# One encoder layer on one core: attention with the values as weights, probabilities scaled before they are transposed, and the modulation pieces spread over two tiles

## What is computed

```python
mod = silu(c) @ ada_w + ada_b                    # 6 x 1024: shift, scale, gate, twice
h = modulate(rms_norm(x, norm1_g), sh1, sc1)
proj = h @ w_in
y_rwkv = rwkv7_time_mix(...)                     # 8 heads of 64, a recurrence over the tokens
y_att = swa_sink_attention(q, k, v, ...)         # 8 query heads, 2 key/value heads of 64
x = x + gt1 * (concatenate([y_rwkv, y_att]) @ w_out)
h2 = modulate(rms_norm(x, norm2_g), sh2, sc2)
x = x + gt2 * hier_moe(h2, ...)                  # 32 experts, two for each token
```

```python
logits = q @ k.T * HEAD_DIM ** -0.5 + bias
probs = softmax(concatenate([logits, sink]))[..., :KEY_BAND]
out = probs @ v
```

## Time and profile before

| | us |
|---|---|
| median of 3 runs | 2782.31 (2781.85 to 2783.21) |
| the profiled execution, its own time | 2783.43 |
| its span in the trace | 2781.5 |
| TensorE busy | 2444.3 (88%) |
| VectorE busy | 1126.3 (40%) |
| ScalarE busy | 755.4 (27%) |
| pass 1 ends, pass 2 begins (from the span's start) | 914.5, 922.8 |

### The profile page before, as it was taken

One profiled execution on the slowest core, in us unless ns is written; L12 is line 12 of the kernel. 1 busy time (PEld: TensorE's weight loads), 2 busy tenths in 40 slices (PEclk: granted clock), 3 DMA queues, 4 the chain that ended last, 5 costly groups with the idle time before them and its releaser, 6 DMA issues. The chain is left out here.

```text
span 2781.5 us, 67296 instructions
## 1 busy us (share of the span) xinstructions
PE 2444.3 (88%) x27710; PEld 1536.3 (55%) x27711; DVE 1126.3 (40%) x2596; ACT 755.4 (27%) x1815; POOL 391.6 (14%) x481
## 2 busy tenths in 40 slices
PE   3999999999997789999999997379999999998970
PEld 1878778788785567677777774223332333232220
DVE  0355645645556245555555554411111111111118
ACT  0244344353443113232323231012122212122212
POOL 0111111111111012121212120001010111110100
PEclk8999999999998799999999998589999999999985
DMA  8012111121123722222222221475535386999959
GB/s 324 9 51 87 47 70 68 47 85 53 46 84 124 305 99 86 101 86 101 86 101 86 101 86 39 185 314 226 219 136 224 138 324 239 384 363 412 373 228 362
DMA packets 54675, 451.78 MB, mean 162 GB/s; under 512 B 7932, under 2 KB 8992, under 8 KB 32576
## 3 DMA queue, kind: packets, MB, share of 16 engines
q1 hardware_dynamic: 36504, 390.71, 35.7%
q0 software_dynamic: 10656, 38.80, 3.6%
q10 hardware_dynamic: 7304, 19.19, 1.9%
HBM read 367.41 MB, written 87.56 MB: 164 GB/s over the span
## 5 line engine op out<-in xcount | busy, mean ns | idle before, releaser
L1729 PE MATMUL ps<-arena 128*32 128x512 f32 x4608 | 510.3, 599 | 27.9 <-DMA arena<-wex 27.9
L1729 PEld LDWEIGHTS ps<-arena 128*32 128x32 f32 x4608 | 150.0, 111 | 381.6 <-issue 358.0
L454 PE MATMUL ps<-arena 128*128 128x128 f32 x3072 | 354.2, 276 | 2.2 <-ACT arena L596 2.1
L454 PEld LDWEIGHTS ps<-arena 128*128 128x128 f32 x3072 | 348.7, 192 | 13.3 <-ACT arena L596 13.3
L1090 PE MATMUL ps<-arena 64*64 64x64 f32 x8704 | 295.2, 220 | 28.6 <-ACT arena L1293 9.2
L1090 PEld LDWEIGHTS ps<-arena 64*64 64x64 f32 x8704 | 275.2, 135 | 57.9 <-issue 56.5
L1743 PE MATMUL ps<-arena 128*32 128x512 f32 x2304 | 268.3, 607 | 15.0 <-DMA arena<-wex 14.1
L1235 PE MATMUL ps<-arena 128*128 128x512 f32 x512 | 238.2, 609 | 0.7 <-ACT arena L1312 0.7
L1951 DVE TENSOR_TENSOR arena<-arena,ps 128x256 f32<-128x256 f32 x72 | 30.0, 416 | 462.5 <-ACT arena L1787 462.5
L465 PE MATMUL ps<-arena 128*128 128x512 f32 (+1 forms) x512 | 216.4, 561 | 0.0
L1787 ACT ACT_TABLE_LOAD x36 | 46.2, 1283 | 592.1 <-PE ps L1729 592.1
(11 more groups left out here) (327 smaller groups left out, 3017.2 us busy)
## 6 DMA issues: line engine op xcount, KB each, us to landing
arena<-wex SPq DMA_DIRECT2D x105, 2048.0 KB
mid<-arena SPq DMA_DIRECT2D x16, 2568.0 KB, 8.5
arena<-mid SPq DMA_DIRECT2D x16, 2568.0 KB, 9.7
arena<-ada SPq DMA_DIRECT2D x12, 2048.0 KB, 10.4
arena<-y SPq DMA_DIRECT2D x16, 1024.0 KB, 8.0
arena<-x SPq DMA_DIRECT2D x31, 512.0 KB, 5.3
arena<-w_in SPq DMA_DIRECT2D x8, 1232.0 KB, 24.8
arena<-x ACTq DMA_DIRECT2D x17, 512.0 KB, 10.8
```

Of the source, the lines that this page charges most:

```text
L454: mm = pe.matmul(bank[name][0:m, at:at + P], V["w_in"][:, kk, w0:w0 + m], V["hT"][:, kk, :], start=(kk == 0), stop=(kk == KD - 1))
L1729: mm = pe.matmul(bank[("HA", "HB")[g]][rows[j], :], xT[:, kk, rows[j]], slot[j][:, at:at + 2 * FH], start=(kk == 0), stop=(kk == KD - 1))
```

## The change

It has four parts.

1. **Values as weights.** In `att5_g` the values (128 keys by 64) are the weights, and the transposed probabilities of two heads (256 columns) stream through. Two heads go to partitions 0 to 63 of C2, two to partitions 64 to 127. There are 4 matmuls for each group, and the result already stands transposed. Pass 2 therefore no longer transposes `ya`: ScalarE copies it straight into `W["yT"]`. The rows of w_out are reordered on the host to fit.
2. **Probabilities scaled first.** The new step `pn_g` on VectorE adds, takes reciprocals and scales the 4 x 192 exponentials of a group in place. `att4_g` waits for it instead of for `probs`. `att4_0` now stands right behind the logits of group 1, ahead of `in_q1`.
3. **Modulation in two rounds.** `mod0` and `mod1` stay in round -1; `mod2` to `mod8` stand in round 0, between the inversion steps of tile 1.
4. **The hand-over.** Pass 1 ends without waiting for its last store. The second ada piece's load and VectorE's first write for `mod0` wait for it instead. w_out is loaded behind the second piece.

```diff
-             ("tok1", 0), ("exp_0", 0), ("in_kv2", 1), ("ev_v", 1), ("tok2", 0), ("ev_l", 1), ("att3_1", 0), ("exp_1", 0),
-             ("in_q1", 1), ("turn_l", 1), ("att4_0", 0), ("in_q2", 1), ("att5_0", 0), ("ev_lora", 1), ("norm", 2),
+             ("tok1", 0), ("exp_0", 0), ("in_kv2", 1), ("ev_v", 1), ("tok2", 0), ("pn_0", 0), ("ev_l", 1), ("att3_1", 0), ("att4_0", 0), ("pn_1", 0), ("exp_1", 0),
+             ("in_q1", 1), ("att5_0", 0), ("turn_l", 1), ("in_q2", 1), ("ev_lora", 1), ("norm", 2),
...
-            sp.wait_ge(S["zero_row"], 16)
-            sp.wait_ge(S["stored"], 16 * nt)
...
-                    S.wait(pe, "probs", 2 * t + g + 1)
+                    S.wait(pe, "pn", 2 * t + g + 1)
...
-                    for i in range(4):
-                        h = 4 * g + i
-                        B.wait_read(pe, f"T{i // 2}", f"P{g}", t)
-                        for part in range(2):
-                            v = V["qkv"][b if part else 1 - b][:, 640 + 64 * g:704 + 64 * g]
-                            mm = pe.matmul(bank["C2"][:, 64 * h:64 * h + 64], V["PT"][:, i, P * part:P * part + P], v,
+                    for half in range(2):
+                        B.wait_read(pe, f"T{half}", f"P{g}", t)
+                    for part in range(2):
+                        v = V["qkv"][b if part else 1 - b][:, 640 + 64 * g:704 + 64 * g]
+                        for half in range(2):
+                            mm = pe.matmul(split(bank["C2"][64 * half:64 * half + 64, 256 * g:256 * g + 256], 2), v,
+                                           V["PT"][:, 2 * half:2 * half + 2, P * part:P * part + P],
                                            start=(part == 0), stop=(part == 1))
...
+            def probs(g):
+                def go(t, b):
+                    S.wait(dve, "probs", 2 * t + g + 1)
+                    g4 = slice(4 * g, 4 * g + 4)
+                    dve.tensor_tensor(V["den"][:, g4], V["sm"][:, g4], V["es"][:, g4], ALU.add)
+                    dve.drain()
+                    dve.reciprocal(V["den"][:, g4], V["den"][:, g4])
+                    dve.drain()
+                    keys = V["Pm_v"][:, :, 64:256]
+                    dve.tensor_tensor(keys, keys, per_channel(V["den"][:, g4], KEYS), ALU.mult).then_inc(S["pn"], 1)
+                return go
...
-                dve.tensor_tensor(split(pk["ya"], QH), split(bank["C2"][:, :], QH), per_channel(V["den"], HD), ALU.mult).then_inc(S["ya"], 1)
+                dve.tensor_copy(pk["ya"], bank["C2"][:, :]).then_inc(S["ya"], 1)
...
+    MODS_FIRST = 2
+
+    def once(step, at):
+        return lambda n, b: step() if n == at else None
 
     def mods(step):
-        return {f"mod{i}": once(lambda i=i: step(i)) for i in range(MODS + 1)}
+        return {f"mod{i}": once(lambda i=i: step(i), 0 if i < MODS_FIRST else 1) for i in range(MODS + 1)}
...
-            for n in range(2):
-                load_ada(sp, S, W["ada"], ins, MOD1 + n)
+            load_ada(sp, S, W["ada"], ins, MOD1)
+            sp.wait_ge(S["stored"], 16 * nt)
+            load_ada(sp, S, W["ada"], ins, MOD1 + 1)
+            sp.dma_start(W["w_out"], ins["w_out"].rearrange("(k p) n -> p k n", p=P)).then_inc(S["w_out"], 16)
...
-                for name, src in (("O1", pk["ya"]), ("O0", W["yc"])):
-                    B.wait_free(pe, name, "yT", t)
-                    if name == "O0":
-                        S.wait(pe, "yr", t + 1)
-                    for c in range(CC):
-                        mm = pe.transpose(bank[name][:, P * c:P * c + P], src[:, P * c:P * c + P], ident)
-                    B.full(mm, name)
+                B.wait_free(pe, "O0", "yT", t)
+                S.wait(pe, "yr", t + 1)
+                for c in range(CC):
+                    mm = pe.transpose(bank["O0"][:, P * c:P * c + P], W["yc"][:, P * c:P * c + P], ident)
+                B.full(mm, "O0")
...
             def yT(t, b):
-                for i, name in ((1, "O1"), (0, "O0")):
-                    B.wait_full(act, name, "yT", t)
-                    B.free(act.activation(W["yT"][:, 4 * i:4 * i + 4, :], split(bank[name][:, :], 4), ACT.Copy), name)
+                S.wait(act, f"pack{b}", 16 * (t // 2) + 16)
+                B.wait_full(act, "O1", "o", t - 1)
+                act.activation(W["yT"][:, 4:KD, :], split(W["pk"][b]["ya"], 4), ACT.Copy).then_inc(S["yaT"], 1)
+                B.wait_full(act, "O0", "yT", t)
+                B.free(act.activation(W["yT"][:, 0:4, :], split(bank["O0"][:, :], 4), ACT.Copy), "O0")
...
+                if i == 0:
+                    dve.wait_ge(S["stored"], 16 * nt)
```

32 lines of the change are left out of this document (15 added, 17 removed), and 7 rows, old and new, of the table ORDER.

## The result

The changed kernel took 2807.33 us (median of 4 runs, 2805.98 to 2807.65), the one before 2782.08 us in the same session (4 runs, 2781.43 to 2783.21): ratio 1.0089, 95% interval 1.0072 to 1.0107, so it is 0.9% slower. The forecast was 2783 with a range from 2766 to 2798. The profiled execution of the changed kernel took 2805.98 us with a span of 2804.2, 22.7 more than the span before.

What follows compares the result with a forecast made beforehand. TensorE's own list plus its waits was taken to bound both passes. Pass 1 +21, its end -10.7, modulation -6.4 and pass 2 -3 summed to +1 us: 2783 us against the median of 2782.3, range 2766 to 2798.

Steps and rivals of the forecast that it cites:

- pass 1 without its end: Pass-1 tiles: values 1.50 us cheaper, new wait 1.25 us dearer, a clock fall in every tile (+24.9); sum +21 us.
- the last tile: End of pass 1: cheaper values at half clock and earlier second transposes outweigh the added scaling; -3 us.
- the wait for the store: End of pass 1: TensorE resumes about 0.8 us after the last store's issue, without waiting for it; -7.7 us.
- modulation, rounds -1 and 0: Early pass 2: piece waits, half-clock stretches and short waits shrink, against some new costs; -6.4 us, bounds -15 and +3.
- pass 2 from round 1: Pass 2: four transposes go, but VectorE's copy limits the recurrence's start to 0.2 us earlier a tile; -3 us, bound -8.
- the one that took the transfers at the hand-over as hidden: End of pass 1: store and first piece share DMA engines, second piece waits, but mod1 comes 28 us later; part of -10.7 us.
- Rival 2: Hand-over: modulation hides wholly in round 0 and the last tile gains more, -10 us further, 2773 us; chance 0.18.
- Rival 3: Pass-1 values: the array halves do not overlap, so each tile loses the 1.50 us gain; +22, 2805 us; chance 0.08.
- The signs of being wrong that the prediction gave: Pass 1: clock stays up behind the new wait, values take 1.8 us, or the wait differs from 2.65 by over 0.5.
- what it expected to see: Profile after: 2.65 us waits, clock falls, values 1.05 us; pass 2 about 11 us sooner; piece waits at most about 2.

Runs made afterwards that it cites:

- e6: Changed kernel plus ten extra 128-column matmuls ahead of group 0's transposes in 15 pass-1 tiles; 41 us faster than the changed kernel, 0.7% faster than before.
- e1: Kernel before with the early hand-over alone; gains nothing (interval leaves 3.3 us at most), stretch to round 1 132.5 us against 124.3.
- e2: Kernel before with the hand-over and the modulation in two rounds, attention as it was; median -1.0 us against e1, not distinguishable.
- e11: Changed kernel with e4's pass-1 order and ten overwritten products ahead of the second group's values in 15 tiles; median 2760.75 us.
- e14: Changed kernel with loads of the second piece, w_out and the gates' bias held back until some 11 us into pass 2; time that of the changed kernel.
- e12: e11 with four modulation pieces in round -1 instead of two; 2757.9 us, ratio 0.9907 to the kernel before.
- e4: Changed kernel with pass 1 reordered, group 0's transposes behind a projection step; ten runs 2766.22 to 2803.31 us, profiled execution 2772.11.
- e8: e4 with the copies of the second group's transposes put ahead of the next tile's norm; median 2779.5 us.
- e10: Changed kernel transferring only an eighth of each of the six last modulation pieces; only the stretch to round 1 read, 124.5 us against 130.0.

## Why the prediction was wrong

Against its own profiled time the forecast's sum was 2784.4; the profiled execution took 2806.0. The 21.6 us come from these terms, as differences of the two traces (their spans differ by 22.7):

```text
                                       forecast   measured
pass 1 without its end                   +21       +21.2
the last tile                             -3        -1.3
the wait for the store                    -7.7      -7.6
round -2                                   0        -0.9
modulation, rounds -1 and 0               -6.4      +6.6
pass 2 from round 1                       -3        +2.5
behind the last o matmul                   0        +2.2
```

**Pass 1 was right.** Forecast: the values -1.50 a tile, the wait 2.65 instead of 1.40, a fall of the clock in each tile at 2.1 us, together +21 ahead of the last tile. Measured: 2 x (1.80 - 1.01) = -1.58, the wait 2.57, 15 falls, +21.2. What a fall costs comes out as 52.77 - (50.86 + 1.17 - 1.58) = 2.3 us, where 50.86 is the old tile without a fall. e6 gives nearly the same without this sum: its tile, with the wait filled and no fall, is 2.1 us shorter. The Trainium skill (TensorEngine Tiling (Array Packing), "Key Properties") has a change of tiling mode drain TensorE and gives no price. The row bears out that it is small: eight passes of 256 columns with a switch in and one out take 1.01 us, and 0.93 had been taken for the passes alone.

**The step that failed is the one that took the transfers at the hand-over as hidden**, and with it the modulation's gain. The hand-over was to give -7.7 and the modulation -6.4. The wait for the store did shrink by 7.6, but rounds -1 and 0 grew by 6.6. In e1, with nothing else changed, the stretch to round 1 grew by 8.2 and the time stayed as it was. I had taken the store and the second piece's load as hidden, since "`mod1` comes 28 us later", and looked at that piece alone. But the DMA engines are 0.9 busy until the last piece has landed, before the change as in e1, and the store now shares that queue. In e1 pass 2 began 9.9 us sooner and the last wait for a piece ended 2.3 us sooner. In the trace of before, the two waits for pieces already said that transfers set round -1. An earlier start in front of such a stretch mostly lengthens its waits. The spreading of the pieces, which was to shorten them, gave -0.8 in e2 against e1.

The kernel before was profiled once, with 124.3 us to round 1. The 13 kernels with the hand-over and all transfers lie between 124.9 and 133.2, and 12 of them at 126.9 or more, so that it grew rests on more than one pair.

Then the parts of -6.4, in the changed kernel. The waits for pieces should have fallen from 4.8 to some 2 us and were 3.6 (0.32 and 3.31). "In round -1 the recurrence loses the matmuls that filled its waits, about +1.2 us": the four waits shown above are 3.2, and before there were none. The waits for instructions were not in the sum at all; they rose from 3.3 to 6.0 in total. A wait of 0.82 for the next tile's load, at the end of round 0, is new too. Half-clock stretches were to go (-3.3): there were 10.2 us of them behind round -2 before, and 13.6 after. The misses, 1.6 + 2.0 + 2.7 + 0.8 + 5.0, make 12.1 of the 13.0 us. All but the last are sums of waits in the rows; the last is an estimate, half of the 3.4 us more of slow clock plus the 3.3 not saved. How much of each wait comes from the others is open.

Rival 2, that the hand-over gives still more, had the sign wrong. Rival 3's 2805 lies next to the result, but by chance: its halves that do not overlap would have left the values at 1.8 us. The signs of being wrong that the prediction gave all lay in pass 1, and none of them came. Of what it expected to see, two things failed, both in the step above: pass 2 began 7.6 us sooner behind the last values and not about 11, and a piece was waited for by 3.31 us and not at most 2.

**Pass 2**: -3 forecast, +2.5 measured in the two profiled executions, of which one fall of the clock is part. Four transposes less gained nothing that can be seen: the first recurrence step starts 2.1 us after the step `Wi` does in both kernels, and TensorE now waits 0.40 for VectorE. I had let it start when VectorE's copy ended, 0.2 us sooner. But it starts 0.26 us after the copy's end before and 0.25 after, and the copy itself waits for the products of `Wi` in both. In the runs of the other kernels here pass 2's remainder lies between 676.8 and 686.4 us with or without the four transposes, so nothing can be claimed of either sign.

**The rest**: the stage behind the last o matmul took 2.2 us longer and is no part of the change; over the kernels here that run it unchanged it took 1049 to 1063 us. The median lies 1.35 us above the profiled execution, where that of before lay 1.1 below.

The verdict follows: pass 1's +20 was seen, and what was to pay for it, 7.7 + 6.4 + 3 = 17 us, came to nothing. What is settled: the clock's share in pass 1 (e6, e11), and that the hand-over alone gains nothing, since the DMA queue behind it ends hardly sooner (e1). What is open: whether the loads make TensorE wait for its instructions (e14 speaks for it, e6 and e12 show it is not all), what the transfers cost the kernel before, since that was not run with them cut, and whether two pieces or four in round -1 are better.

## What to carry to other kernels

Price a new wait of TensorE by the clock behind it as well as by its length, and try to fill it with work that nobody needs before reordering around it: ten products a tile turned 0.9% slower into 0.7% faster, and with the new order and an even split into 0.9% faster. Before counting a shortened wait as a gain, follow the DMA queue to the next place where the engine waits for a transfer: if the DMA engines are busy all the way there, those transfers do not land earlier, and the gain ends there. Before moving matmuls out of a stretch with short waits, price them at both places: here six pieces saved 14.1 us where they had stood and added 19.6 where they went.

## What the runs showed of the hardware

Two halves of the array with 64 columns each, all 128 rows in use, ran eight passes of 256 columns in 1.01 us, with a switch of shape on either side.

Equal waits did not give equal falls of the clock. In the changed kernel waits of 2.57 us gave slow stretches of 3.4 and 6.8 us in turn. With waits of 1.79 us, 2.15 in two tiles, the clock fell once in the profiled execution (e4), and the runs of that kernel spread over 37 us; waits of 0.87 and 0.94 in every tile gave stretches of 10.2 us in four of 15 (e8). The Trainium skill (TensorE: Matmul & The Clock Gate, Part 1: The HAM clock gate) says that what the chip looks at is free-running, not tied to the kernel. The alternation agrees with it; that the spread of the runs comes from it was not shown.

While transfers kept the DMA engines 0.9 busy at some 360 GB/s, 2.6 MB more in the same stretch took about 8 us more (before and e1).

TensorE waited up to 4.35 us with nothing in the rows but "issue" as its reason (e4; 3.84 in e2 and e10), where the DMA engines were full of loads.
